# Delta rule: another order of VectorE's and ScalarE's work within a step

## What is computed

```
gc = cumsum(g)
decay = exp(where(tril, gc[:, None] - gc[None, :], -inf))
m = where(strict, (k * beta) @ k.T * decay, 0)
tmat = inverse(m + eye)                       # triangular
u = tmat @ (v * beta);  w = tmat @ (k * beta * exp(gc))
qk = (q @ k.T) * decay
v_new = u - w @ s
o = (q * exp(gc)) @ s + qk @ v_new
s = s * exp(gc[-1]) + (k * exp(gc[-1] - gc)).T @ v_new
```

## Time and profile before

| | |
|---|---|
| median of 3 runs | 3141.66 us |
| the profiled execution | 3141.73 us, span 3139.9 us |
| TensorE busy | 2968.0 us (95%) |
| VectorE busy | 1669.5 us (53%) |
| ScalarE busy | 1214.1 us (39%) |
| GpSimd busy | 309.4 us (10%) |
| granted TensorE clock, mean | 0.972 of 2.4 GHz |

### The profile page before, as it was taken

One profiled execution on the slowest core, in us unless ns is written; L12 is line 12 of the kernel. 1 busy time (PEld: TensorE's weight loads), 2 busy tenths in 40 slices (PEclk: granted clock), 3 DMA queues, 4 the chain that ended last, 5 costly groups with the idle time before them and its releaser, 6 DMA issues.

```text
span 3139.9 us, 53876 instructions
## 1 busy us (share of the span) xinstructions
PE 2968.0 (95%) x22796; PEld 2420.2 (77%) x22796; DVE 1669.5 (53%) x2942; ACT 1214.1 (39%) x2193; POOL 309.4 (10%) x449
## 2 busy tenths in 40 slices
PE   7999999999999999978889999999999999999998
PEld 4767787766777688778766788888888877788887
DVE  3245666455533656677755553555556636554444
ACT  4315435356441455433345552111114437642221
POOL 1010020000001000043330010111110101000000
PEclk9999999989999999988889999999999999999999
DMA  6285542210314722001020022333342341032321
GB/s 230 81 296 183 187 156 89 94 55 18 106 69 173 264 101 71 22 18 29 24 69 28 1 74 81 124 120 119 121 146 76 93 75 48 8 107 101 107 94 67
DMA packets 180585, 308.11 MB, mean 98 GB/s; under 512 B 24038, under 2 KB 58151, under 8 KB 180089
## 3 DMA queue, kind: packets, MB, share of 16 engines
q1 hardware_dynamic: 141408, 253.87, 24.2%
q0 software_dynamic: 12048, 40.24, 4.2%
q10 hardware_dynamic: 26889, 10.56, 1.2%
HBM read 296.47 MB, written 6.81 MB: 97 GB/s over the span
## 4 chain that ended last, share of the span: by engine, by line
PE 78%; DVE 12%; ACT 6%; DMA 2%; issue 1%; POOL 0%; ACTq 0%; DVEq 0%; POOLq 0%
PE psum L428 20%; PE psum L429 20%; PE psum L430 20%; PE psum L1229 2%; DVE weights_r L370 2%; PE psum L2723 2%; PE psum L1257 1%; PE psum L1245 1%; DMA weights<-in_w_mod 1%; PE psum L621 1%; PE psum L2713 1%; DVE arena L917 1%; PE psum L1006 1%; PE psum L2825 1%; PE psum L1040 1%
## 5 line engine op out<-in xcount | busy, mean ns | idle before, releaser
L370 DVE TENSOR_TENSOR weights_r<-weights,weights_r 128x2048 fp32r<-128x2048 f32 (+1 forms) x161 | 360.5, 2259 | 379.9 <-ACT weights_r L361 379.9
L361 ACT ACTIVATE weights_r<-weights 128x2048 fp32r<-128x2048 f32 (+1 forms) x161 | 302.4, 1896 | 649.2 <-DMA weights<-in_w_ffn_gate 218.9
L428 PE MATMUL psum<-feat_r,weights_r 128*128 128x512 f32 (+1 forms) x1536 | 540.0, 352 | 1.2 <-ACT arena L2498 1.0
L429 PE MATMUL psum<-feat_r,weights_r 128*128 128x512 f32 (+1 forms) x1536 | 537.5, 350 | 0.0
L430 PE MATMUL psum<-feat_r,weights_r 128*128 128x512 f32 (+1 forms) x1536 | 536.7, 349 | 0.0
L428 PE MATMUL psum<-weights_r,feat_r 128*128 128x512 f32 (+2 forms) x1344 | 522.4, 389 | 12.1 <-DVE feat_r L762 8.8
L430 PE MATMUL psum<-weights_r,feat_r 128*128 128x512 f32 (+2 forms) x1344 | 517.4, 385 | 0.0
L429 PE MATMUL psum<-weights_r,feat_r 128*128 128x512 f32 (+2 forms) x1344 | 516.9, 385 | 0.0
L428 PEld LDWEIGHTS psum<-feat_r,weights_r 128*128 128x128 f32 x1536 | 294.4, 192 | 44.4 <-issue 5.4
L430 PEld LDWEIGHTS psum<-feat_r,weights_r 128*128 128x128 f32 x1536 | 293.9, 191 | 37.1
L429 PEld LDWEIGHTS psum<-feat_r,weights_r 128*128 128x128 f32 x1536 | 294.4, 192 | 36.3
(11 more groups left out here) (534 smaller groups left out, 4284.0 us busy)
## 6 DMA issues: line engine op xcount, KB each, us to landing
weights<-in_w_mod SPq DMA_DIRECT2D x30, 2048.0 KB, 16.6
weights<-in_gla_w_in SPq DMA_DIRECT2D x24, 1024.0 KB, 7.4
arena<-in_w_mod_turned POOLq DMA_DIRECT2D x96, 256.0 KB, 3.2
weights<-in_w_ffn_gate SPq DMA_DIRECT2D x22, 1024.0 KB, 6.9
weights<-in_w_ffn_up SPq DMA_DIRECT2D x22, 1024.0 KB, 5.1
weights<-in_w_ffn_down SPq DMA_DIRECT2D x20, 1024.0 KB, 6.9
weights<-in_fox_w_in SPq DMA_DIRECT2D x16, 1024.0 KB, 6.7
weights<-in_sgu_w_in SPq DMA_DIRECT2D x12, 1024.0 KB, 6.6
```

Of the source, the lines that this page charges most:

```text
L361: act.e.activation(WEI_r[:, s * SLOT + HALF:s * SLOT + HALF + n], WEI_t[:, s * SLOT:s * SLOT + n], ACT.Copy).then_inc(*A.put(("weights", c ...
L370: dve.e.tensor_tensor(WEI_r[:, s * SLOT:s * SLOT + n], WEI_t[:, s * SLOT:s * SLOT + n], WEI_r[:, s * SLOT + HALF:s * SLOT + HALF + n].bitc ...
L428: pe.e.matmul(ps, lh, rh, start=first, stop=False)
L429: pe.e.matmul(ps, lh, rl, start=False, stop=False)
```

## The change

In VectorE's step, dif and clamp are no longer done at the end for step n + 2 but in the next step, for n + 1: dif behind e 0, clamp behind the state. The merge's first g comes before the state. The second e comes before kk. In ScalarE's step, join z, cross and the load come before Relu of step n + 1, and its Exp comes behind the second et. The whole diff:

```
--- before.py
+++ after.py
@@ -2984,14 +2984,14 @@
             act_et(act, n, 0)
             if behind:
                 act_join_v(act, n - 1)
-            if more:
-                act_decay_relu(act, n + 1)
-                act_decay_exp(act, n + 1)
-            if behind:
                 act_join_z(act, n - 1)
                 act_cross(act, n - 1)
                 act_rows(act, n + 2)
+            if more:
+                act_decay_relu(act, n + 1)
             act_et(act, n, 1)
+            if more:
+                act_decay_exp(act, n + 1)
             if behind:
                 act_corner(act, n - 1)
             if more:
@@ -3152,13 +3152,17 @@
         for n in range(STEPS):
             more, behind = n + 1 < STEPS, n > 0
             dve_e(dve, n, 0)
+            if more and behind:
+                dve_dif(dve, n + 1)
+            dve_g(dve, n, 0)
             dve_state(dve, n)
-            dve_g(dve, n, 0)
+            if more and behind:
+                dve_clamp(dve, n + 1)
             dve_x(dve, n, 0)
+            dve_e(dve, n, 1)
             if more:
                 dve_kk(dve, n + 1, 0)
                 dve_kk(dve, n + 1, 1)
-            dve_e(dve, n, 1)
             dve_g(dve, n, 1)
             dve_qk(dve, n)
             dve_x(dve, n, 1)
@@ -3170,9 +3174,6 @@
                 dve_s(dve, n - 1)
                 dve_o(dve, n - 1)
             dve_vb(dve, n)
-            if n + 2 < STEPS:
-                dve_dif(dve, n + 2)
-                dve_clamp(dve, n + 2)
         for t in ALL[3::2]:
             dve_mla_down(dve, t)
         dve_mla_begin(dve)
```

More of the change, by code:

```diff
@@ L2986, in act_gdn @@
                 act_join_v(act, n - 1)
[L2987 to L2990, removed]
                 act_join_z(act, n - 1)
```

## The result

The changed kernel takes 3218.0 us, the median of four runs (3209.93 to 3230.46), beside 3142.39 of the kernel before on the same chip: a ratio of 1.0236, 95% interval 1.0210 to 1.0263. The forecast was 3164.0 with a range up to 3178. Slower was right, and so was the wait that causes it; the size, +22.3, was less than a third of what came. The profiled execution took 3214.66 us with a span of 3212.9, that is 72.93 more than the one before.

What follows compares the result with a forecast made beforehand. TensorE, 78% of the last chain, and a twelve-step chain of engines waiting for each other were taken as the bound. Steps 4 to 10 +11.0, steps 1 and 2 +8.1, step 0 +1.9, step 3 +1.3: +22.3 on 3141.73, 3164.0 us, range 3141 to 3178.

Steps and rivals of the forecast that it cites:

- e ahead of dif and clamp: Head of a middle step: e2 starts 3.3 us after zero in place of 5.1; TensorE's 1.82 us wait goes.
- VectorE sets x at 7.9 or 8.5: First half: VectorE's queue, not TensorE, sets x at 7.9 us after zero, 8.5 where dif takes 2.29; mean 8.15.
- kk needs exp, kq1 needs kk's banks, 2.55 a step: Second half: kk, behind exp, ends at X + 6.0 for X + 3.4 (X: x's start), delaying kq1; 2.55 us a step.
- The clock in the second half: From kq1 to x: TensorE's 3.1 us wait lowers the clock; price 2.0 us a step, bounds 0 and 2.2.
- the slow stretch of the first half goes: First half of a middle step: the low-clock stretch behind the wait for e disappears, already counted in the 8.15 us.
- C: Rival: both halves of the step at low clock, +2.3 us in nine steps, 3184.7 us; chance 0.05.
- at 0.50 nearly throughout: Step 3: runs at low clock behind a stop, so later kk costs 0 to 2.55 us, taken as 1.3.
- A: Rival: clock stays at 2.4 GHz over the new kq1 wait, 2.0 us less in nine steps, 3146.0 us; chance 0.18.
- B: Rival: kk's end stays hidden from kq1 on TensorE, a middle step takes 19.35 us, total 3117.2 us; chance 0.14.
- At no cost: GpSimd's blocks, 2.6 us later with kk, the decay rows' load and the reads of decays d add no time.

Runs made afterwards that it cites:

- the three faster kernels: Changed kernel with kk back ahead of e, clamp behind dif, Relu and Exp ahead of cross: 0.9972; that plus products ahead of both et: 0.9977; or plus kq0 moved: 0.9977.

## Why the prediction was right and wrong

**e ahead of dif and clamp: right.** e2 came at 3.25 in steps 2 and 4, with no wait for L3078. TensorE's waits by what ended them (us in total, times, longest), before and after:

```profile
PE psum L2723 <- DVE feat L3078: 20.7, 11, 2.9
...
PE psum L2713 <- DVE feat L3047: 0.8, 2, 0.4
```

```profile
PE psum L2713 <- DVE weights L3047: 26.5, 7, 4.0
PE psum L2713 <- DVE feat L3047: 10.8, 3, 4.0
...
PE psum L2723 <- DVE feat L3078: 2.3, 1, 2.3
```

18.4 us of one wait went, and the other grew to 37.3.

**VectorE sets x at 7.9 or 8.5: right while the clock was up** (7.79 in step 2, 8.51 in step 4), wrong from step 5 on, 12.17.

**kk needs exp, kq1 needs kk's banks, 2.55 a step: right.** (The terms given for the end of exp, 0.9 + 1.06 + 0.65 + 1.06, add up to X + 3.67 and not 3.75; nothing turns on it.) kk at 3.48 behind x in step 2, released by L2906, and a kq1 wait of 2.83. Where kq0 is issued two places later, so that its banks are not the next ones of kq1, the wait is gone. In the settled steps kk comes later (4.66 behind x), since its chain runs through e2g, cross and et, at lower clock too.

**The clock in the second half, "the bounds are 0 and 2.2": the step that failed.** Its direction was right: the wait of 2.83 was followed by 0.50. But I put a price on the stretch from kq1 to x alone, bounded it by the slowest such stretch of the kernel before, and wrote off the first half ("the slow stretch of the first half goes"). It did not go. TensorE, slow from kq1 on, is late with u, s and o, so it enters the next step behind and still at 0.50, and has no idle time until e2. Measured in a settled step the term is 1.6 more behind kq1, 4.0 in the first half, 0.8 ahead of kk. Over seven steps that is 45 us of the same matmuls at lower clock, where the whole forecast for these steps was 11.0. Of the 8.80 us behind step 10, forecast as nothing, some may come in the same way: the first 10 us of step 11 are at 0.50, and TensorE has no idle time in them.

```profile
1646.73:1656.73 10.00, 10.00 (x251) 9.70 (x252) 3.66 (x10) 1.30 (x4) 2.77 (x5) 0.50 0.30 120
```

But five kernels of the experiments have the same order of work as the changed kernel from step 11 on, and took 1559.6 to 1566.4 us from its zero to the end of the span, for 1566.1; so no run shows how much of the 8.80 the change itself makes.

**The rivals.** C, both halves at low clock, named the right mechanism with a chance of 0.05 and a price of 3184.7, still 30 short of the profiled 3214.66. It took its price from e2 to x in step 10 and left e2 itself at 3.3. A whole step of such a state stood in the earlier trace rows: step 3 of the kernel before took 1423.71 - 1393.51 = 30.20, and the settled steps took 30.67. Seven steps at 30.20 would have come to 53.0 over the 158.44; 52.34 were measured. I had called step 3 such a state and did not use its length. That it fits so well is partly luck. The granted clock of step 3 is 0.66, near the settled 0.61 (the prediction's "at 0.50 nearly throughout" says too much), but its length also holds a stop of 4.26 us in the middle of join v, which the settled steps don't have; they have 3.9 us of kq1's wait for kk instead, which step 3 doesn't.

```profile
1393.96:1424.16 30.20, 25.27 (x608) 23.51 (x608) 17.03 (x40) 7.81 (x15) 9.98 (x16) 0.66 0.07 20
```

```profile
1399.55 0.48 PE L2768 MATMUL psum<-feat,weights 32*32 32x32 f32 x4 [4.26 <-issue]
```

A, the clock staying up, is wrong as a forecast (0.50 behind 2.83 us), but the run with added products shows its terms to be about right at full clock. By the rule of the Trainium skill that stands behind A (TensorE: Matmul & The Clock Gate, "Loop structure matters more than you think"), the time would have been A's 3146.0. This trace speaks against it where TensorE stands and waits: the granted clock was 0.50 behind the wait of 2.83 us for VectorE's kk. B is wrong by kq1's waits: kk's end was not hidden. The kernel that keeps kk ahead of e comes nearest to B's time, at 0.9972.

**At no cost: right**, as far as the runs go. GpSimd's blocks and the load of the decay rows end none of TensorE's long waits, and GpSimd and ScalarE are as busy in steps 4 to 10 as before.

**What stays open.** Why the clock falls in kernels whose kq1 waits for kk hardly (0.86 with kk ahead of e) or not at all (0.75 with kq0 moved), and not behind every wait; why the state of low clock, once there, settles at 30.7 a step while the kernel with kq0 moved takes 23.7 without settling; why the three faster kernels don't come nearer to 19.35 a step; and what the 0.3 to 0.4% are made of that the two kernels with kq0 moved and kk late still lose.

## What to carry to other kernels

Before a reader of a rotating buffer is moved later, list who opens that slot next: here the next one was kq1, with five more groups of matmuls queued behind it, and it had no use for kk's result. When a wait on TensorE is followed by a lower clock, price the whole loop at that clock, first half included. A step of the same kernel that already runs so is a better start for the price than one stretch of it, once what else its length holds is taken out. If the order has to stay, moving the write to the slot (here kq0) by two places can loosen the tie.

## What was unexpected of the hardware

Added work made a kernel faster: with five whole-array products in the gap ahead of kq1 the granted clock over steps 4 to 10 was 0.93 in place of 0.63 and the ratio 1.0086 in place of 1.0236. With the corner products issued four times instead, TensorE was busy for 179.33 of 191.47 us and the clock was 0.76; the two runs differ in the size of the added products, in their number and in when they ran, and which of these counts is not shown. And a loop whose steps 4 to 10 differed by over 4 us before (20.88 to 25.19) settled, at a mean granted clock of about 0.61, on a period that six steps kept within 0.6 us.
